# Two of four depthwise-convolution tiles moved from VectorE to GpSimd in a two-layer hybrid decoder (MLA, Conformer convolution, SSD) on one Trainium2 core

## What is computed

```python
def hybrid_layer(x, ...):
    h = rms_norm(x, norm_g)
    u = h @ w_in
    c_q, c_kv, k_pe, g_mla, u_conv, g_conv, z, xbc, dt_raw = split(u)
    o_mla  = mla_mixer(c_q, c_kv, k_pe, ...) * silu(g_mla)      # 6 heads, causal
    o_conv = conformer_conv_mixer(u_conv, ...) * silu(g_conv)
    o_ssd  = ssd_mixer(z, xbc, dt_raw, ...)                     # 12 heads, chunks of 128
    return x + concat([o_mla, o_conv, o_ssd]) @ w_out

def conformer_conv_mixer(u, w_dw, b_dw, ln_g, ln_b, w_pw):      # 512 channels
    a, g = u[..., :512], u[..., 512:]
    h = a * sigmoid(g)
    h = causal_depthwise_conv(h, w_dw, b_dw)                    # 31 taps
    h = silu(layer_norm(h, ln_g, ln_b))
    return h @ w_pw
```

## Time and profile before

| | us |
|---|---|
| median of 3 runs | 1723.15 |
| lowest of 3 runs | 1721.0 |
| profiled execution: span from the first to the last instruction | 1719.0 |
| TensorE / VectorE / ScalarE / GpSimd busy in it | 1575.8 / 1093.9 / 611.8 / 48.8 |

### The profile page before, as it was taken

The page is one execution under the profiler, slowest core; times in us unless marked ns, Lnnn a source line. Parts: engine busy times, 40 slices in busy tenths (PEclk is TensorE's granted clock), DMA queues, the critical chain, the costliest instruction groups (busy, mean ns, idle before and its releaser), DMA issues.

```text
span 1719.0 us, 21432 instructions
## 1 busy us (share of the span) xinstructions
PE 1575.8 (92%) x7062; PEld 1248.2 (73%) x7062; DVE 1093.9 (64%) x1777; ACT 611.8 (36%) x847; POOL 48.8 (3%) x94
## 2 busy tenths in 40 slices
PE   4999999999989878999979999899999898779997
PEld 3877777777767666788867777677777686658885
DVE  6435765888999655544364457658889985563443
ACT  7344443333333233311243445433443332241110
POOL 0000000000000000011000000000000000001110
PEclk9999999999999889999989999999999998899999
DMA  6522222222223213344322222212113232224441
GB/s 217 161 92 77 87 85 67 67 68 67 81 80 102 83 56 95 112 147 147 130 93 82 85 77 98 73 63 74 62 62 101 80 102 67 68 76 148 147 147 61
DMA packets 45173, 162.73 MB, mean 95 GB/s; under 512 B 5600, under 2 KB 6016, under 8 KB 44544
## 3 DMA queue, kind: packets, MB, share of 16 engines
q1 hardware_dynamic: 37440, 133.96, 24.1%
q0 software_dynamic: 7616, 27.32, 5.2%
HBM read 152.82 MB, written 12.63 MB: 96 GB/s over the span
## 4 chain that ended last, share of the span: by engine, by line
PE 60%; DVE 19%; ACT 10%; issue 8%; DMA 1%; DVEq 1%; ACTq 0%; SPq 0%; POOLq 0%
PE acc L470 17%; PE acc L471 16%; PE acc L472 16%; ACT whi L706 3%; DVE cacc L951 3%; DVE xb L896 3%; PE S L475 2%; ACT sqh L696 2%; DVE wlo L903 2%; ACT L696 1%; ACT temp L696 1%; DVE sqh L887 1%; DVE xg L887 1%; PE S L470 1%; DVE xg L896 1%
## 5 line engine op out<-in xcount | busy, mean ns | idle before, releaser
L470 PE MATMUL acc<-hhi,whi 128*128 128x512 f32 (+1 forms) x1824 | 737.5, 404 | 71.7 <-DVE hlo L964 33.1
L471 PE MATMUL acc<-hlo,whi 128*128 128x512 f32 (+1 forms) x1824 | 719.9, 395 | 0.0
L472 PE MATMUL acc<-hhi,wlo 128*128 128x512 f32 (+1 forms) x1824 | 719.4, 394 | 0.0
L903 DVE TENSOR_TENSOR wlo<-stage,whi 128x1024 fp32r<-128x1024 f32 (+3 forms) x252 | 300.8, 1197 | 465.3 <-ACT whi L706 461.8
L470 PEld LDWEIGHTS acc<-hhi,whi 128*128 128x128 f32 (+1 forms) x1824 | 347.8, 191 | 154.3 <-DVE hlo L964 33.7
L706 ACT ACTIVATE whi<-stage 128x1024 fp32r<-128x1024 f32 (+3 forms) x252 | 260.4, 1037 | 543.2 <-PE acc L472 455.3
L472 PEld LDWEIGHTS acc<-hhi,wlo 128*128 128x128 f32 (+1 forms) x1824 | 346.7, 190 | 76.8
L471 PEld LDWEIGHTS acc<-hlo,whi 128*128 128x128 f32 (+1 forms) x1824 | 347.8, 191 | 75.1 <-issue 4.4
L951 DVE SCALAR_TENSOR_TENSOR cacc<-glu,pv,cacc 128x512 f32<-128x512 f32 x240 | 171.8, 749 | 13.4 <-DVE temp L896 1.9
L696 ACT ACTIVATE prob<-S,cols 128x128 f32<-128x128 f32 (+3 forms) x48 | 25.4, 528 | 135.0 <-DVE cols L891 135.0
L696 ACT ACTIVATE temp<-temp 128x512 f32<-128x512 f32 x48 | 30.3, 631 | 107.4 <-DVEq L883 107.4
(11 more groups left out here) (212 smaller groups left out, 1325.8 us busy)
## 6 DMA issues: line engine op xcount, KB each, us to landing
stage<-weights SPq DMA_DIRECT2D x236, 512.0 KB, 3.6
xr<-y_features POOLq DMA_DIRECT2D x32, 256.0 KB, 3.6
y_features<-xg POOLq DMA_DIRECT2D x32, 256.0 KB, 3.4
acsb<-acs_rows POOLq DMA_DIRECT2D x16, 384.0 KB, 4.2
xg<-x_features SPq DMA_DIRECT2D x4, 1024.0 KB, 8.9
y_features<-x_features POOLq DMA_DIRECT2D x8, 512.0 KB, 3.7
stage<-weights SPq DMA_DIRECT2D x8, 256.0 KB, 2.8
stage<-weights SPq DMA_DIRECT2D x4, 384.0 KB, 3.1
```

Source lines behind the costliest of these rows:

```text
L470: nc.tensor.matmul(out, a, c, start=start, stop=False)
L471: nc.tensor.matmul(out, a, d, start=False, stop=False)
L472: return nc.tensor.matmul(out, b, c, start=False, stop=stop)
L903: nc.vector.tensor_tensor(wlo[u % RING][:, 0:w], stage[u % STAGE][:, 0:w], whi[u % RING][:, 0:w].bitcast(F32), ALU.subtract).then_inc(lo_d ...
```

## The change

The constructor of the signals and buffers gets three new signals: `glu_ready` (a tile of glu complete, 4 per layer), `pool_prod` and `pool_tap` (2 x 31 per layer each). VectorE's list of taps has only tiles 2 and 3 left (62 in each layer) and is opened at tile 21 in place of tile 17. GpSimd makes tiles 0 and 1, ahead of its wait for the first `acsb` load. Each tap but the first is a scaled copy of the shifted input to `xg[:, 9, :]` and, after a wait for it, an addition into `cacc`; the next scaled copy waits for that addition. The first tap of a tile is a multiply and add. The pad of `glu` grows from 30 to 32 columns, and every tap reads two columns further on. VectorE waits for all of GpSimd's taps before it evacuates gconv 0.

```diff
-        PADC = CONV_K - 1
+        PADC = CONV_K + 1
+        POOL_TILES = (0, 1)
...
+            def pool_conv(layer):
+
+                n = 0
+                for j in POOL_TILES:
+                    pool.wait_ge(glu_ready.sem, glu_ready.at(layer, j + 1))
+                    for k in range(CONV_K):
+                        src = glu[:, j, k + 2:k + 2 + SEQ]
+                        wt = pv[:, PARAM_COLS["dww"][0] + CONV_K * j + k:PARAM_COLS["dww"][0] + CONV_K * j + k + 1]
+                        wb = pv[:, PARAM_COLS["dwb"][0] + j:PARAM_COLS["dwb"][0] + j + 1]
+                        if n:
+                            pool.wait_ge(pool_tap.sem, pool_tap.at(layer, n))
+                        n += 1
+                        go()
+                        if k == 0:
+                            nc.gpsimd.tensor_scalar(cacc[:, j, :], src, wt, wb, ALU.mult, ALU.add).then_inc(pool_tap.sem, 1)
+                            pool.sem_inc(pool_prod.sem, 1)
+                        else:
+                            nc.gpsimd.tensor_scalar(xg[:, 9, :], src, wt, None, ALU.mult).then_inc(pool_prod.sem, 1)
+                            pool.wait_ge(pool_prod.sem, pool_prod.at(layer, n))
+                            nc.gpsimd.tensor_tensor(cacc[:, j, :], cacc[:, j, :], xg[:, 9, :], ALU.add).then_inc(pool_tap.sem, 1)
...
                         if s == 0:
+                            pool_conv(layer)
 
                             pool.wait_ge(o_taken.sem, o_taken.at(layer, 24))
...
-                taps = [(j + i, k) for j in (0, 2) for k in range(CONV_K) for i in range(2)]
+                taps = [(2 + i, k) for k in range(CONV_K) for i in range(2)]
 
                 def convolve(n):
 
-                    for _ in range(min(n, len(taps))):
+                    for _ in range(min(n, len(taps)) if taps_open[0] else 0):
...
-                    if name == "in" and args == (17, 0):
+                    if name == "in" and args == (21, 0):
                         taps_open[0] = True
...
                                 dve.wait_ge(scores_done.sem, scores_done.at(layer, 24))
+                                dve.wait_ge(pool_tap.sem, pool_tap.at(layer, 2 * CONV_K))
                             evac(j, temp[:, :], half=True)
...
-                            silu(None, glu[:, i, PADC:PADC + SEQ], glu[:, i, PADC:PADC + SEQ])
+                            silu(glu_ready, glu[:, i, PADC:PADC + SEQ], glu[:, i, PADC:PADC + SEQ])
```

More of the change, by code:

```diff
@@ L166 @@
 NPAR = _at
-ACT_CHAIN, DVE_CHAIN = 32, 358
+ACT_CHAIN, DVE_CHAIN = 32, 354
 NCONST = 2 * SEQ + 3 * P
@@ L379, in hybrid_kernel @@
         branch_ready = sig("branch_ready", 6)
-        tap_done = sig("tap_done", 4 * CONV_K)
+        tap_done = sig("tap_done", 2 * CONV_K)
+        glu_ready = sig("glu_ready", 4)
+        pool_prod = sig("pool_prod", 2 * CONV_K)
+        pool_tap = sig("pool_tap", 2 * CONV_K)
         act_chain = sig("act_chain", ACT_CHAIN)
@@ L937, in _ @@
                 taps_open = [False]
-                taps = [(j + i, k) for j in (0, 2) for k in range(CONV_K) for i in range(2)]
+                taps = [(2 + i, k) for k in range(CONV_K) for i in range(2)]
                 def convolve(n):
-                    for _ in range(min(n, len(taps))):
+                    for _ in range(min(n, len(taps)) if taps_open[0] else 0):
                         j, k = taps.pop(0)
-                        src = glu[:, j, k:k + SEQ]
+                        src = glu[:, j, k + 2:k + 2 + SEQ]
                         wt = par("dww", CONV_K * j + k)
@@ L948, in convolve @@
                         else:
-                            dve.wait_ge(tap_done.sem, tap_done.at(layer, CONV_K * 4 - len(taps) - 2))
+                            dve.wait_ge(tap_done.sem, tap_done.at(layer, CONV_K * 2 - len(taps) - 2))
                             ins = nc.vector.scalar_tensor_tensor(out=cacc[:, j, :], in0=src, scalar=wt,
@@ L1176, in _ @@
                         convolve(len(taps))
-                        dve.wait_ge(tap_done.sem, tap_done.at(layer, 4 * CONV_K))
+                        dve.wait_ge(tap_done.sem, tap_done.at(layer, 2 * CONV_K))
                         tt(None, csum[:, :], cacc[:, 0, :], cacc[:, 1, :], ALU.add)
```

## The result

The changed kernel takes 1778.35 us (median of 4 runs, 1776.4 to 1778.99) against 1722.99 for the kernel before: a ratio of 1.0327, 95% interval 1.0311 to 1.0342, or 55.4 us slower. The forecast was 1764 with a range of 1709 to 1816. The direction was right, and so was the mechanism except for how long one instruction holds up the other; the size was a quarter short: 41 us of the 55.

What follows compares the result with a forecast made beforehand. TensorE was taken to bound the kernel (92% busy), with VectorE's order setting the pace in stretch B. Per layer +25 - 5 = +20 us, both layers +40, on a span of 1719: 1759, as median 1764, range 1709 to 1816.

Steps and rivals of the forecast that it cites:

- A: Layer 0, 293 to 360.6 us, attention beside the last ua/ug tiles: taps fill idle VectorE time, removing them gains nothing.
- B: Layer 0, 360.6 to about 482 us, attention then SSD beside xbc tiles: VectorE sets the pace; net loss 25 us.
- C: Layer 0, 482.8 to 551 us, SSD with the last 21 cacc instructions: losing them gains 5 us (0 to 7).
- GpSimd's price: Per GpSimd tap, copy 0.81 and addition 1.03 us: 1.85 us of work (1.23 to 2.46), 2.31 with waits.
- The hold: In stretch B, GpSimd instructions block two-SBUF-input VectorE instructions for their whole length: 21 x 1.85 x 0.73 = 28.4 us lost.
- The Trainium skill's rule: Shared SBUF ports: VectorE instructions with two SBUF inputs contend with GpSimd's SBUF reads; the later one blocks fully.
- GpSimd in time: GpSimd's taps start at 258.4 us and end near 434, before its first acsb load at 454.6 us.
- Rival 2: GpSimd late: acsb load behind the convolution delays ssd_a 0 if taps average over 3.6 us; 1817 us, chance 0.15.
- Rivals 1 and 3: The first: engines don't hinder each other, 1709 to 1713 us, chance 0.26; the other: a real gain, chance 0.03.
- rival 3: A real gain of over 2%, needing 34 us, 17 per layer; chance 0.03.

Runs made afterwards that it cites:

- e1: Changed kernel with 30 of the 31 taps of tiles 0 and 1 on GpSimd left out, only each first kept: 1715.07 us, ratio 0.996.
- e4: Changed kernel with taps 15 to 30 of tiles 0 and 1 left out, the rest begun on GpSimd at 259 us: 1720.51 us.
- e5: Changed kernel with taps 15 to 30 of tiles 0 and 1 left out, GpSimd begun only at 358 us: 1758.45 us, ratio 1.0203.
- e10: Changed kernel with GpSimd's 60 scaled copies per layer left out, its additions begun only at 358 us: 1788.97 us.
- e7: Changed kernel, all work done, with GpSimd begun after glu tile 1 (296 us) in place of tile 0 (259 us): 1824.84 us.
- e11: Changed kernel with GpSimd's 60 additions per layer left out, its scaled copies begun only at 358 us: 1771.93 us.

## Why the prediction came out as it did

- *What bounds the kernel, and A, B, C.* Right. A is free (taking its taps away gained at most 0.5 us in e1, and GpSimd's work there cost nothing in e4 and the changed kernel), B is VectorE's, C gave 2.7 us in the changed kernel and 3.8 in e1, where I took 5 between 0 and 7. The tiles of C fell only to 15.1 us (520.08 to 535.18), not to the 13.9 of a tile without xbc work, which was the wrong partner to compare with.
- *GpSimd's price.* The first mis-sized term. I had 0.81 for the copy, with 1.09 as the upper end, and 1.03 for the addition. Measured with little contention are 1.56 and 1.28 us. The copy, the simpler of the two, is the dearer, and twice VectorE's row was no bound for it. A tap took 3.4 us before B, not 2.5, so 32 additions fell into B, not 21 taps' worth.
- *The hold.* The second mis-sized term, to the other side. The upper end of the two bounds, the full length of every GpSimd instruction, gives 1.85 x 0.73 = 1.35 us per tap; measured are 29.5 / 32 = 0.92 in the changed kernel and 0.73 in e5. A hold does not last as long as the instruction: it ends 0.98 us into an addition and 0.50 into a copy, and what arrives later loses less or nothing, so a copy costs 0.14 us on average. The two errors nearly cancel, 32 x 0.92 against 21 x 1.35, so that B came to 29.5 and not 25: close, and partly by luck.
- *The Trainium skill's rule* (SBUF — State Buffer, Who interferes with whom) is borne out in which VectorE instructions suffer: two SBUF inputs 748 to 1164 ns, one from PSUM 692 before and after. That the later one waits and isn't merely slowed is borne out too (the e10 rows). The Trainium skill says there, of VectorE's two-port modes, that whoever issues first has the pair for the whole instruction, and the prediction took the same for GpSimd's instructions. That isn't what the runs show: a copy of 1.59 us lets VectorE go after 0.50. A VectorE instruction with one SBUF input, the first tap of a tile, was held up too (rows at the end); the Trainium skill excludes that only outside VectorE's two-port modes, and no run shows which mode this one was in.
- *Before A.* The term I left out. I counted from 293 us, but GpSimd begins at 259, where VectorE has six rotation instructions with two SBUF inputs on attention's path (2.2 us longer together) and a wlo right behind them (2.21 us in place of 1.22, 0.7 of it lost). That is 2.9 us per layer; the other shortfalls are 4.5 in B and 2.3 in C.
- *GpSimd in time.* Right in outcome, with far less room than stated: I had its end near 434 us, it was 479. Rival 2's mechanism is real (e7 and e11), and its point was well placed: 62 taps took (479.1 - 259.2) / 62 = 3.55 us each against a stated 3.6.
- *Rivals 1 and 3* fell: VectorE's instructions in B lengthened, and without any GpSimd cost at all the change gains 7 us (e1), so the 34 us that rival 3 needs weren't there to gain.

Sum of the corrections per layer: B 29.5 for 25, rotation 2.9 for 0, C 2.7 for 5, so 29.7 for 20, and 59 for 40; the span grew by 57.7 and the median by 55.4.

Left open: why a tap of GpSimd costs 0.92 us in the changed kernel and 0.73 in e5. In the former the two engines fall into a fixed rhythm (tiles of 22.2 us, one after another, with the same instruction, the silu of xb, at 1789 ns each time); that the rhythm makes the difference wasn't tried.

## What to carry over

Before moving work to an idle engine, ask what the work costs where it lies now: in A the taps were free on VectorE, in C they were worth 3 to 4 us per layer, and 7 us of 1723 was all there was to gain. Then price the move in time of the busy engine: a GpSimd tap took 0.73 to 0.92 us of VectorE's time in B, and VectorE's own tap takes 0.75, so even in time it saved nothing. An idle queue may also be idle because something urgent comes behind: here 8 us separated a hidden convolution from one that delays the next stage.

## What was unexpected of the hardware

- On GpSimd the scaled copy of 128x512 float32 (`tensor_scalar` with a multiply and a column scalar) takes 1.56 us at least, the addition of two such tensors 1.09 at least and 1.28 in the median. The multiply-add with two column scalars (L443) took 0.77 us at the start of tile 1, half of the multiply alone. The Trainium skill (GPSIMD Engine Reference, 4.1 Engine selection) calls one-input work roughly line-rate and two-input work some twice slower than VectorE's. The multiply-add and the addition agree with that order (0.77 and 1.28 us); the multiply alone, the longest of the three, doesn't.
- Beside a busy VectorE an addition costs it 0.63 us on average, the longer copy 0.14: VectorE's instructions with two SBUF inputs are let go about 0.98 us after an addition began (e10) and 0.50 us after a copy began (e11).
- VectorE's `tensor_scalar`, with one tensor input from SBUF, takes 938 ns (median) beside GpSimd's taps and 542 without them. The same line, after and then e1 (duration min/median/max):

```profile
L973 DVE TENSOR_SCALAR cacc<-glu,pv x4: 917/938/958, 363.6 to 1238.7; 128x512 f32<-128x512 f32 x4
```

```profile
L973 DVE TENSOR_SCALAR cacc<-glu,pv x4: 540/542/543, 360.9 to 1204.2; 128x512 f32<-128x512 f32 x4
```

- TensorE was idle for 20% of B, and its mean granted clock there was 0.89 of the full one; in A, where it had no gap, 1.00.
